# A hybrid decoder step on one core: padded row picking, scaling moved to ScalarE, and a spread product of ones with diagonals

## The reference, cut to what matters

```python
# mixer, HGRN2 group, for each of the 8 samples and 4 heads (one new token each):
S_new = exp(b_last)[..., None] * S + einsum('bshk,bshv->bhkv', k_dec, vc)   # 128 x 128 state
...
x = x + m                          # output projection added, 1024 wide
h = rmsnorm(x, norm2_g[l])         # x * rsqrt(mean(x*x) + eps) * g
# layer 1:
logits = (t @ router_w)            # 264 tokens x 8 experts
top_v, top_i = lax.top_k(logits, 2)
probs = softmax(top_v)
out = sum over experts e of gates[:, e] * swiglu(t, w1[e], w3[e], w2[e])
```

## Time and profile before

| | us |
|---|---|
| median of 3 runs (lowest, highest) | 1561.75 (1560.56, 1565.26) |
| the profiled execution, its own time | 1560.95 |
| its span in the profile | 1559.1 |
| layer 0's mixer, end of its projection to the next norm | 148 to 176 |
| layer 1's mixer, chunk loop | 504 to 533 |
| router, turning and picking | 533 to 564 |
| expert phase | 564 to 1545 |

### The profile page before, as it was taken

How to read it: one execution, slowest core, us unless ns; L and a number is a source line. 1 busy time by engine, 2 the same in 40 slices (tenths; PEclk the granted TensorE clock), 3 DMA queues, 4 the chain that set the end, 5 groups by cost and what they waited for, 6 DMA issues and landing times.

```text
span 1559.1 us, 23107 instructions
## 1 busy us (share of the span) xinstructions
PE 1517.3 (97%) x8415; PEld 1303.4 (84%) x8415; DVE 1255.6 (81%) x1245; ACT 963.5 (62%) x811; POOL 72.6 (5%) x75
## 2 busy tenths in 40 slices
PE   6999899998999999999999999999999999999996
PEld 5999899998999778888888888888888888888884
DVE  5886775667686848888888889888889889889897
ACT  4446444345446447777776777777677777777774
POOL 3000100000000210000000000000000000000000
PEclk9998999999998979999999999999999999999999
DMA  9541555554441469999999999999999999999992
GB/s 295 186 136 55 199 192 199 175 187 135 158 132 44 161 229 386 383 354 384 371 352 384 377 354 375 374 359 378 369 363 363 378 368 359 377 382 347 376 393 105
DMA packets 215730, 447.98 MB, mean 287 GB/s; under 512 B 7529, under 2 KB 63265, under 8 KB 215417
## 3 DMA queue, kind: packets, MB, share of 16 engines
q1 hardware_dynamic: 208176, 421.59, 75.2%
q0 software_dynamic: 6368, 23.38, 4.0%
q10 hardware_dynamic: 1136, 2.36, 0.4%
HBM read 433.98 MB, written 13.39 MB: 287 GB/s over the span
## 4 chain that ended last, share of the span: by engine, by line
PE 94%; DVE 4%; issue 1%; ACT 1%; DMA 0%; DVEq 0%; SPq 0%
PE ps L1515 28%; PE ps L1516 27%; PE ps L1517 27%; PE ps L1577 2%; PE ps L1856 2%; PE ps L1657 1%; DVE w_lo L864 1%; PE ps L1826 1%; PE ps L1677 1%; PE ps L1531 1%; PE ps L1666 0%; PE ps L1596 0%; PE ps L1816 0%; PE ps L1786 0%; PE ps L1525 0%
## 5 line engine op out<-in xcount | busy, mean ns | idle before, releaser
L864 DVE TENSOR_TENSOR w_lo<-raw,w_hi 128x2048 fp32r<-128x2048 f32 x401 | 911.6, 2289 | 180.0 <-ACT w_hi L545 172.4
L545 ACT ACTIVATE w_hi<-raw 128x2048 fp32r<-128x2048 f32 x401 | 763.1, 1917 | 234.1 <-PE ps L1517 232.3
L1515 PE MATMUL ps<-w_hi,xg 128*128 128x512 f32 x896 | 359.1, 401 | 0.0
L1517 PE MATMUL ps<-w_hi,xg 128*128 128x512 f32 x896 | 354.3, 395 | 0.0
L1516 PE MATMUL ps<-w_lo,xg 128*128 128x512 f32 x896 | 354.2, 395 | 0.0
L1515 PE MATMUL ps<-h_hi,w_hi 128*128 128x264 f32 x736 | 215.4, 293 | 17.1 <-DVE h_lo L891 15.1
L1517 PE MATMUL ps<-h_hi,w_lo 128*128 128x264 f32 x736 | 211.1, 287 | 0.0
L1516 PE MATMUL ps<-h_lo,w_hi 128*128 128x264 f32 x736 | 210.9, 287 | 0.0
L1517 PEld LDWEIGHTS ps<-w_hi,xg 128*128 128x128 f32 x896 | 168.3, 188 | 40.6
L1515 PEld LDWEIGHTS ps<-w_hi,xg 128*128 128x128 f32 x896 | 168.5, 188 | 38.9
L1516 PEld LDWEIGHTS ps<-w_lo,xg 128*128 128x128 f32 x896 | 168.6, 188 | 37.8
(11 more groups left out here) (297 smaller groups left out, 1414.0 us busy)
## 6 DMA issues: line engine op xcount, KB each, us to landing
raw<-in_moe_w_dram SPq DMA_DIRECT2D x336, 1024.0 KB, 6.9
raw<-in_ffn_w_dram SPq DMA_DIRECT2D x33, 1024.0 KB, 5.4
raw<-in_w_in_dram SPq DMA_DIRECT2D x24, 1024.0 KB, 5.8
raw<-in_w_out_dram SPq DMA_DIRECT2D x8, 1024.0 KB, 5.3
hstate<-in_state_hgrn_dram POOLq DMA_DIRECT2D x2, 2048.0 KB, 12.3
out_dram<-hstate POOLq DMA_DIRECT2D x2, 2048.0 KB, 9.4
y_rows<-y_f POOLq DMA_DIRECT2D x4, 512.0 KB, 4.8
y_pair<-y_rows POOLq DMA_DIRECT2D x2, 1024.0 KB, 10.6
```

What stands on the lines that cost most here:

```text
L545: act.activation(w_hi[:, s, :], raw[:, r, :], ACT.Copy).then_inc(hi_made, 1)
L864: dve.tensor_tensor(w_lo[:, s, :], raw[:, r, :], w_hi[:, s, :].bitcast(F32), ALU.subtract).then_inc(split, 1)
L1515: pe.matmul(out, l_hi, r_hi, start=start, stop=False)
L1517: return pe.matmul(out, l_lo, r_hi, start=False, stop=stop)
```

## The change

Five things are done. **(1)** The spread of a sample's values becomes one product: the ones as weights, and as the moving side a 128 x 512 tile `diag` that holds, for each head, the identity times the value column. GpSimd writes it (`spread_out`), three samples ahead of TensorE, into three places over the memory of `v_tok`. **(2)** In layer 1, ScalarE makes `hF` (a copy with a scale for each partition), one chunk ahead of that chunk's square, in place of VectorE. **(3)** The router's base is written by GpSimd in `sum_squares`; `slot_row` is still filled by VectorE, later. **(4)** The picking uses all 128 rows of the third tile; GpSimd clears `h_tok`'s third part first, and ScalarE waits for that (`rest_cleared`). **(5)** The last two state updates of layer 1 move: that of sample 6 behind the margin, that of sample 7 behind the first picks, and TensorE waits for all updates at chunk 4 of the picking. GpSimd's queue is reordered: final state's store, three diagonals, four small stores, then the rest.

```diff
k_tok = at("k_tok", places["zq"], [2, HEADS, P])
         s_fin = at("s_fin", places["zx"], [HEADS, P])
+        diag = at("diag", places["sc"], [3, HEADS, P])
...
@@ GpSimd @@
-            def store_rows(l):
+            def store_final(l):
                 pool.wait_ge(fin_ready, l + 1)
                 pool.dma_start(hgrn_prompt[l, 0].rearrange("h k v -> k h v"), s_fin[:, :, :]
                                ).then_inc(fin_stored, 16)
+
+            def spread_out(l, b):
+                if b >= 3:
+                    pool.wait_ge(kv_done, NSAMPLE * l + b - 2)
+                else:
+                    pool.wait_ge(vs_ready, l + 1)
+                pool.tensor_tensor(diag[:, b % 3, :, :],
+                                   ident[:, None, :].broadcast_to([P, HEADS, P]),
+                                   v_s[:, :, b:b + 1].broadcast_to([P, HEADS, P]), ALU.mult
+                                   ).then_inc(diag_ready, 1)
+
+            def store_rows(l):
                 pool.wait_ge(rows_ready, l + 1)
...
             def sum_squares():
+                pool.wait_ge(fin_stored, 16 * DEPTH)
+                for place_of, value in ((rt[:, :, :, :], 0.0), (small[:, 144:150], 1.0),
+                                        (tok_row[:, :, :, :], 1.0)):
+                    link(pool.memset(place_of, value))
+                for t in range(3):
+                    link(pool.tensor_scalar(tok_row[:, t, :, 0], tok_row[:, t, :, 1],
+                                            tok_ids[:, t:t + 1], None, ALU.mult))
+                link(pool.tensor_scalar(spare_row, tok_ids[:, 0:1], 2.0 * T, None, ALU.add))
+                pool.sem_inc(base_made, 1)
                 pool.wait_ge(sq_ready, 3 * DC + 1)
                 for c in range(1, DC):
+                    if c + 2 < NSAMPLE:
+                        spread_out(DEPTH - 1, c + 2)
                     pool.wait_ge(sq_ready, 3 * DC + c + 1)
...
                 pool.sem_inc(sq_summed, 1)
+                pool.memset(h_tok[:, 2, :], 0.0).then_inc(rest_cleared, 1)
...
                                ).then_inc(st_landed, 16)
+                store_final(l)
+                for b in range(3):
+                    spread_out(l, b)
+                store_rows(l)
                 if l == DEPTH - 1:
-                    store_rows(l)
                     sum_squares()
+                else:
+                    for b in range(3, NSAMPLE):
+                        spread_out(l, b)
                 pool.wait_ge(st_new, NSAMPLE * HEADS * (l + 1))
...
-                if l < DEPTH - 1:
-                    store_rows(l)
@@ ScalarE @@
             for c in range(DC):
                 act.wait_ge(x_sum, 16 + 8 * FF_STEPS + c + 1)
+                act.activation(hF[:, c, :], xT[:, c, :], ACT.Copy,
+                               scale=vecT[:, V_N2 + DC + c:V_N2 + DC + c + 1]).then_inc(h_full, 1)
                 act.activation(sq[:, c, :], xT[:, c, :], ACT.Square).then_inc(sq_ready, 1)
...
             act.wait_ge(fin_stored, 16 * DEPTH)
+            act.wait_ge(rest_cleared, 1)
@@ VectorE @@
-            def router_base():
...
-                    if l == DEPTH - 1:
-                        dve.wait_ge(x_sum, 16 + 8 * FF_STEPS + c + 1)
-                        dve.tensor_scalar(hF[:, c, :], xT[:, c, :], v(V_N2 + DC + c), None,
-                                          ALU.mult).then_inc(h_full, 1)
-                        if c == 4:
-                            router_base()
+                    if l == DEPTH - 1 and c == DC - 1:
+                        return new_state
                     if l < DEPTH - 1:
                         new_state(c)
                     elif c:
                         new_state(c - 1)
-                    if l == DEPTH - 1 and c == DC - 1:
-                        return lambda: new_state(c)
...
-            last_state = mixer(1)
+            new_state = mixer(1)
+            dve.wait_ge(base_made, 1)
             dve.wait_ge(logits_done, 1)
...
-            last_state()
+            new_state(NSAMPLE - 2)
...
             make_pick(0, 0)
+            new_state(NSAMPLE - 1)
...
+            dve.tensor_copy(slot_row[:, 0:1], spare_row).then_inc(rows_known, 1)
@@ TensorE @@
-                    for h in range(HEADS):
-                        ins = pe.matmul(ps[:, 5 + b % 3, P * h:P * h + P],
-                                        v_s[:, h, b:b + 1].broadcast_to([P, P]), ident[:, :],
-                                        start=True, stop=True)
-                    ins.then_inc(kv_done, 1)
+                    pe.wait_ge(diag_ready, NSAMPLE * l + b + 1)
+                    pe.matmul(ps[:, 5 + b % 3, :], ones[:, :],
+                              diag[:, b % 3, :, :].rearrange("p h v -> p (h v)"), start=True,
+                              stop=True).then_inc(kv_done, 1)
...
                 for c in range(DC):
-                    for t, _, n in TOKEN_TILES:
+                    if c == 4:
+                        pe.wait_ge(st_new, DEPTH * NSAMPLE * HEADS)
+                    for t in range(3):
                         ins = pe.matmul(ps[:, 5 + c // 4, P * (c % 4):P * (c % 4) + P],
-                                        h_tok[0:n, t, c * P:(c + 1) * P], pick[0:n, t, :],
+                                        h_tok[:, t, c * P:(c + 1) * P], pick[:, t, :],
                                         start=(t == 0), stop=(t == 2))
```

More of the change, by code:

```diff
@@ L250, in trunk @@
             sem("base_ready"))
+        diag_ready = sem("diag_ready")
+        base_made, rest_cleared = sem("base_made"), sem("rest_cleared")
         chosen_ready, pos_done, blocks_ready = (sem("chosen_ready"), sem("pos_done"),
@@ L946, in _ @@
             b3 = lambda a: a[:, :, 0:1].broadcast_to([P, 3, EXPERTS])
-            def router_base():
-                link(dve.memset(rt[:, :, :, :], 0.0))
-                link(dve.memset(small[:, 144:150], 1.0))
-                link(dve.memset(tok_row[:, :, :, :], 1.0))
-                for t in range(3):
-                    link(dve.tensor_scalar(tok_row[:, t, :, 0], tok_row[:, t, :, 1],
-                                           tok_ids[:, t:t + 1], None, ALU.mult))
-                link(dve.tensor_scalar(spare_row, tok_ids[:, 0:1], 2.0 * T, None, ALU.add))
-                dve.tensor_copy(slot_row[:, 0:1], spare_row).then_inc(rows_known, 1)
             def mixer(l):
```

## The result

The changed kernel is slower: 1565.44 us (median of 9 runs, 1562.89 to 1566.77) against 1560.56 for the kernel before on the same chip (9 runs, 1553.02 to 1565.26), ratio 1.0045 [1.0026, 1.0065]; and once more 1564.35 against 1556.18 (35 runs), ratio 1.0044 [1.0027, 1.0060]. The forecast was 1557.3. The profiled execution took 1565.15 us, its span is 1563.4.

The account below looks back on a forecast made before the run. TensorE, busy 97% of the span, was taken to bound the kernel. Terms -0.5 + 4.0 + 2.4 + 0.3 - 8.3 - 2.4 = -4.5 us took the median from 1561.75 to 1557.3; own range 1553.8 to 1560.5, with two rivals 1553.0 to 1563.8.

Parts of the forecast that it names:

- GpSimd's diagonals. ... Cost: 0.: Both layers: GpSimd writes each diagonal in about 1.8 us, in time for TensorE's spreads, so nothing is lost.
- rival (c): Samples 3 to 7 of layer 1: GpSimd late with its diagonals, about 15 us, 1572; chance 0.06.
- Rival (f): Layer 0: GpSimd's products slow VectorE by a tenth over five diagonals, 0.9 us, 1558.2; chance 0.02.
- No row here shows VectorE slowed: Remark on VectorE and GpSimd sharing SBUF interfaces: the profile rows show no VectorE slowing; no size given.
- Spread product, -0.5: Both layers: one 512-column product of 0.87 us replaces four taking 0.89, weight loads go; -0.5 us (0 to -1).
- Stall, +4.0: Layer 1's first router product: TensorE waits once for ScalarE's scaling, behind a weight split and table load; +4.0 us.
- Clock lost by it, +2.4: TensorE's work behind the wait at the first router product runs partly at half clock; +2.4 us (0 to 3.2).
- the tail of 0.3: End of layer 1's chunk loop: last square and sum come later, moving L1769's products and logit transposes; +0.3 us (0 to 0.5).
- VectorE's lighter load and moved updates, 0: Layer 1 loop and picking: VectorE loses scalings, base and an update, but TensorE sets the pace and moved updates are hidden; 0.
- Padded picking, -8.3 and -2.4 behind it: Picking at L1826: no stops and full clock returning, 14.69 to 6.4 us, -8.3; the 4.85 us behind it halve, -2.4.
- at the picking as it is, with its stops, it never came back: Picking before the change: full clock did not return during its 14.69 us, supporting the padding's gain.

Follow-up runs that it names:

- scale_dve: Changed kernel with the eight hF scalings back on VectorE, diagonals, GpSimd base and padded picking kept; 1557.53 us, ratio 1.0007 to before.
- act_first: Changed kernel, diagonals included, with ScalarE scaling chunks 0 and 1 on both sides of its last weight split, ahead of the table load; 1557.97 us, ratio 1.0014 to before.
- diag_early: Changed kernel with each layer's first three diagonals written before m_lo, to a buffer of their own; 1563.83 us, ratio 1.0055 to before.
- diag_scalar: Changed kernel with scaling on VectorE and each diagonal written by four one-input GpSimd multiplications, whole result computed; 1561.28 us, ratio 1.0035 to before.
- diag_one_input: Changed kernel with each diagonal made by one GpSimd multiplication by one value per partition, heads 1 to 3 left out; 1557.65 us, ratio 0.9976 to before.
- diag_memset: Changed kernel with GpSimd filling each diagonal with 0.5, reading nothing, the samples' head values left out; 1557.81 us, ratio 0.9984 to before.
- no_diag: Changed kernel with the four products per sample back and no GpSimd diagonals; 1558.18 us, ratio 0.9998 to before.
- after_again: The changed kernel, unchanged, measured again; 1564.35 us, against 1556.18 for the kernel before, ratio 1.0044.
- pad_base: Changed kernel without diagonals and with scaling on VectorE; padded picking, GpSimd base and moved state updates stay; 1550.91 us, ratio 0.9961 to before.
- pad_only: Kernel before with the padded picking alone, plus GpSimd's clearing of h_tok's last part that it needs; 1550.89 us, ratio 0.9972 to before.
- before_again: The kernel before, unchanged, profiled once more; median 1558.34 us, ratio 0.9996 to before, its profiled execution 1553.34 us.
- diag_twice: Changed kernel with every GpSimd diagonal product made twice; 1565.84 us, ratio 1.0031 to before.

## Why the prediction was wrong, point by point

- **The step that failed: "GpSimd's diagonals. ... Cost: 0."** The argument asked only when GpSimd would be through, and not what it does to VectorE meanwhile. Measured +6.2 to +6.6 us: 3.0 in layer 0, 2.4 in layer 1 up to the chunk loop, the rest not placed. The product takes 1.05 us, not the 1.8 assumed, and in the changed kernel TensorE never waits for it, so rival (c) stayed away. Where the stall is gone diagonal 3 of layer 1 is late once, by 0.6 and 1.1 us (scale_dve, act_first); the step has 0.2 for that. Large waits for a diagonal are in diag_early (2.5 us) and, as read above, in diag_scalar (2.95).
- **Rival (f), "VectorE is slowed by GpSimd's products"**, was the right mechanism with the wrong size. "A slowing of a tenth" was a guess, where the bound from above would have been standing still: 16 products of 1.8 us. It was looked for in VectorE's busy share in layer 0's loop; 4.9 us of it came from the first three diagonals, which fell on `m_lo` before the loop, for which TensorE waits (2.4 us at L1538 above). The Trainium skill, GPSIMD Engine Reference, section 8, names contention for VectorE's instructions with two SBUF inputs. The trace agrees on which VectorE instructions stand, and its sizes are 1.46 to 4.74 and 0.69 to 2.57 us. That GpSimd's one-input scaling does little of it is what diag_one_input shows. "No row here shows VectorE slowed" is so, but one shows GpSimd slowed by VectorE: the sum of 1.03 us in the earlier trace rows.
- **Spread product, -0.5:** it takes 0.86 and 0.87 us for its two records in layer 0's chain, as worked out, and 1.05 behind a router product. diag_memset and diag_one_input have it with nearly no collision, and their layer 0 takes 40.54 and 40.40 us against 40.41 in no_diag: no gain that can be told.
- **Stall, +4.0:** 4.2 measured, for the reason given. **Clock lost by it, +2.4:** (1 - 0.68) x 9.83 = 3.1 in the profile of the changed kernel; in after_again's the clock is 0.57 over the 4 us from 517 and 1.00 behind, 1.7 us lost. Runs give 6.3 to 7.3 for the part, where the forecast has 6.7 with the tail of 0.3. Right.
- **VectorE's lighter load and moved updates, 0:** pad_base and pad_only are level. Right, as far as their spread tells.
- **Padded picking, -8.3 and -2.4 behind it:** this is the second step that failed, by its size. 14.69 became 5.93 (6.4 forecast; 0.91 on the mean is 1.1 us at half clock, 2.2 forecast) and 3.48 became 1.81. Against the execution profiled first pad_only gave -10.6 where the step says -10.7. But in the medians it is 4.2 to 5.3 us: in before_again the clock is back ahead of the picking, and two thirds of the executions of before lie in its heap. The step "at the picking as it is, with its stops, it never came back" took one execution for all; at full clock the stops cost 8.24 - 5.36 = 2.9 us. Which execution was profiled could not be told from the three times shown, all of the upper heap.
- **The end:** 0.5 and 10.7 gained and 6.7 lost were to give -4.5. Against medians it is -5.3 + 6.6 + 6.8 = +8.2 (1556.18 to 1564.35, by the ratio +6.9). The forecast stood on 1561.75, the upper heap, so its gain by the padding and its starting point were too high together and nearly cancel: with 6.4 for the diagonals its own sum gives 1563.7, 0.7 to 1.7 under the two medians. That it comes so near is in part luck. Without the diagonals the kernel takes 1558.18, which is inside the stated range, and yet it is level with before (0.9998) and not 4.5 us faster.

Open: why before's clock stays low through the picking in one profiled execution and not in the other. In all the other profiles the half clock around the picking lasts at most 7 us (540.3 to 543.7 in before_again), at whatever time they came there.

## What to carry to other kernels

Before work goes to an idle GpSimd, look for VectorE's instructions with two SBUF inputs that run at that time and are waited for, and count each two-input GpSimd instruction that meets them as a delay of up to its own length, once; what falls into a wait that VectorE has anyway is not paid (diag_twice). If it must be there, put it where VectorE waits or reads PSUM. When work moves to another engine's queue, read what stands in that queue at that time: placing two scalings ahead of a table load was worth 6.4 us by the medians. And before a gain is taken from a stretch at half clock, compare the profiled execution with the spread of the times: here it came from a heap that holds 41 of 124 executions.

## What the runs showed of the hardware that was not expected

- The exclusion is not symmetric. VectorE's two-input instructions stand through the whole of GpSimd's two-input products; its one-input scalings hold the one that is at work when they begin, by 0.6 us at most, its fills not at all (0.43 us as ever in diag_memset). GpSimd stands for VectorE's long splits with either: a product took 1.05 us alone and 2.19 behind a split, and three scalings of 128x9 with one input took 3.30 us at 516.69, beside a split of 2.28 from 517.10, and 1.67 in diag_early, where no split ran.
- On GpSimd a product of two broadcast inputs (128x512, 1.05 us) is quicker than a multiplication by one value per partition of the same size (1.59 at the median), and that quicker than four of 128x128 (0.63 each at the median); a fill takes 0.54. Medians of diag_memset, diag_one_input and diag_scalar:

```profile
L444 POOL MEMSET diag<- x16: 524/538/546, 144.4 to 529.3; 128x512 f32 x16
```

```profile
L444 POOL TENSOR_SCALAR diag<-ident,v_s x16: 1554/1590/3445, 144.0 to 529.5; 128x512 f32<-128x512 f32 x16
```

```profile
L445 POOL TENSOR_SCALAR diag<-ident,v_s x64: 592/625/2712, 144.0 to 539.8; 128x128 f32<-128x128 f32 x64
```

- At one and the same clock, full, 48 picking records with a change of operand rows took 8.24 us and padded 5.36: 15 stops of 0.19 us each, 0.23 at half clock by the earlier trace rows.
